# Splitting the expert gathers of a product-key layer into u rows and v rows, and taking two of nine token tiles dense

## The reference, cut to what matters

```
q = xb @ w_query                          # 8 heads x 2 halves x 128
s = q . sub_keys ; sv, si = top_k(s, 16)  # 128 keys in each half
cand = sv0 + sv1 ; fv, fi = top_k(cand, 16)
eidx = si0 * 128 + si1 at fi              # 16 experts per head
g = softmax(fv)
u = expert_u[eidx] ; a = u . xb           # (token, slot)
w = g * gelu(a)
out = sum over slots of w * expert_v[eidx]
```

## Time and profile before

| | us |
|---|---|
| median of 3 runs | 3683.47 (3682.42 to 3684.99) |
| profiled execution, its span | 3684.3 |
| before the first indirect transfer | 729.2 |
| one tile of the second part | 325.4 |

### The profile page before, as it was taken

How to read it: one execution, slowest core, us unless ns; L and a number is a source line. 1 busy time by engine, 2 the same in 40 slices (tenths; PEclk the granted TensorE clock), 3 DMA queues, 4 the chain that set the end, 5 groups by cost and what they waited for, 6 DMA issues and landing times.

```text
span 3684.3 us, 48012 instructions
## 1 busy us (share of the span) xinstructions
PE 3158.2 (86%) x17895; PEld 1389.9 (38%) x17895; DVE 2311.1 (63%) x6107; ACT 719.1 (20%) x2373; POOL 1110.6 (30%) x1177
## 2 busy tenths in 40 slices
PE   6999999889888878988887898889788888977776
PEld 3545556634334324423432343344234334422222
DVE  1333343867757866775776677677667757765444
ACT  2434434311111111111111111111111111111111
POOL 0000000033333333333333333333333333333332
PEclk8999999799999999999999999999999999999999
DMA  5000114299999999999999999999999999999997
GB/s 217 24 29 23 35 34 169 91 401 421 421 421 419 418 414 417 413 414 420 415 414 420 416 414 415 417 418 416 412 417 416 416 416 418 413 414 420 419 418 326
DMA packets 192682, 1275.60 MB, mean 346 GB/s; under 512 B 21056, under 2 KB 24768, under 8 KB 44608
## 3 DMA queue, kind: packets, MB, share of 16 engines
q0 software_dynamic: 165888, 1208.03, 79.4%
q1 hardware_dynamic: 26560, 64.49, 4.9%
HBM read 1260.12 MB, written 12.32 MB: 345 GB/s over the span
## 4 chain that ended last, share of the span: by engine, by line
DMA 46%; PE 35%; DVE 9%; issue 5%; POOL 4%; ACT 1%; SPq 0%; DVEq 0%; POOLq 0%; ACTq 0%
DMA arena<-in_experts,arena 45%; PE PS L1353 10%; PE PS L1182 8%; PE PS L1367 7%; POOL arena L651 4%; DVE arena L976 4%; PE PS L1276 3%; PE PS L1166 2%; PE PS L1399 2%; PE PS L1265 1%; PE PS L1225 1%; DVE arena L1051 1%; DVE arena L1054 1%; DVE arena L1057 1%; PE PS L1205 0%
## 5 line engine op out<-in xcount | busy, mean ns | idle before, releaser
L1353 PE MATMUL PS<-arena 128*128 128x512 bf16 x6912 | 1655.6, 382 | 453.1 <-DVE arena L976 440.6
L976 DVE CUSTOM_DVE_ANT_0 arena<-arena,PS 128x1024 f32<-128x1024 f32 x1152 | 1396.2, 1221 | 871.7 <-DMA arena<-in_experts,arena 548.4
L651 POOL DMA_INDIRECT arena<-in_experts,arena x1152 | 1089.0, 945 | 1938.0 <-PE PS L1367 1572.7
L1353 PEld LDWEIGHTS PS<-arena 128*128 128x128 bf16 x6912 | 611.5, 98 | 1480.5 <-DVE arena L976 865.1
L1367 PE MATMUL PS<-arena 128*32 128x512 f32 x4608 | 558.8, 603 | 16.8 <-ACT arena L867 16.8
L861 ACT ACTIVATE arena<-arena 128x4 f32<-128x4 f32 x288 | 59.5, 207 | 2156.2 <-DVE arena L976 2137.0
L1182 PE MATMUL PS<-arena 128*128 128x512 f32 (+1 forms) x720 | 309.8, 567 | 13.9 <-DMA arena<-in_w_in 7.9
L1399 PEld LDWEIGHTS PS<-arena 128*128 128x128 f32 x2304 | 266.6, 192 | 101.5 <-issue 101.5
L1399 PE MATMUL PS<-arena 128*128 128x128 f32 x2304 | 289.7, 280 | 0.0
L867 ACT ACTIVATE arena<-arena 128x1 f32<-128x1 f32 x1152 | 245.5, 284 | 9.4
L1367 PEld LDWEIGHTS PS<-arena 128*32 128x32 f32 x4608 | 120.8, 109 | 313.9 <-issue 175.4
(11 more groups left out here) (124 smaller groups left out, 1526.8 us busy)
## 6 DMA issues: line engine op xcount, KB each, us to landing
arena<-in_experts,arena POOLq DMA_INDIRECT x1152
arena<-in_w_in SPq DMA_DIRECT2D x8, 1024.0 KB, 11.8
arena<-in_w_query SPq DMA_DIRECT2D x4, 2048.0 KB, 16.1
arena<-in_xT SPq DMA_DIRECT2D x9, 512.0 KB, 3.9
h_scratch<-arena SPq DMA_DIRECT2D x9, 512.0 KB, 2.9
arena<-h_scratch SPq DMA_DIRECT2D x9, 512.0 KB, 8.1
out<-arena SPq DMA_DIRECT2D x9, 512.0 KB
arena<-in_x_prompt SPq DMA_DIRECT2D x8, 512.0 KB, 3.5
```

What stands on the lines that cost most here:

```text
L651: pool.indirect_dma_start(out=uv[r], out_offset=None, in_=experts, in_offset=bass.IndirectOffsetOnAxis(ap=expert_T[t % 2][:, tok:tok + 1], ...
L976: dve.tensor_tensor_reduce(uv[r][:, 0:D], uv[r][:, 0:D], xb(n), 1.0, 0.0, ALU.mult, ALU.add, a_dot[(n // 4) % 2][:, n % 4:n % 4 + 1]).then ...
L1353: mm = pe.matmul(PS[:, 2 + 2 * (n % 2) + c, :], pick[:, tok:tok + 1].broadcast_to([P, P]), parts[t % 2][k][:, 512 * c:512 * c + 512], star ...
```

## The change

It replaces the second part. Seven tiles (`D_TILES`, 0 to 6) are gathered in another way, and two (`PAIR`, 7 and 8) aren't gathered at all. The work is dealt over 256 units of four slots or four tokens, with 35 more at the end for the v side.

- **u by slot.** One indirect transfer takes, for one slot, the u rows of all 128 tokens (4 KB each, 0.5 MB). Tokens lie on the partitions, so `dot` multiplies by `xrow`, the x rows of the tile in SBUF. `spread_x` and the bf16 splits go. x rows are stored to a scratch tensor (`store_x2`) and loaded again by SP (`load_row`), h rows are loaded twice (`load_h`, `load_residual`). The routing of later tiles runs ahead of the gathers.
- **v by token.** When the 128 slots of a tile are done, gelu and gates are one operation each, PE turns the weights, and 35 units behind the u side POOL issues one indirect transfer for each token (128 v rows, 0.5 MB) into eight buffers. ACT writes the four weights of a unit in one copy (`spread_weights`). `weigh_experts` is as before.
- **Two tiles dense.** From unit 151 on, in two halves of 64 expert blocks each: 16 units in which DVE makes one-hot tiles (`spots`: four scaled comparisons of 128x128 and one of 128x256 for four tokens), PE multiplies them (`scatter`), and ACT copies the gates into the matrix `G`. Then 35 units with 64 blocks: SP streams a block of 128 experts of U (turned by the host) and of V, 0.5 MB each, into rings of three, `dense_dots` (8 matmuls of 256 columns), gelu on ACT, `gate_dense` on DVE, `dense_values` (4 matmuls of 512 columns), all float32. The u gathers end with unit 223, the v gathers with 258, the blocks with 252.

```diff
-                    for o in range(SLOTS):
-                        n = t * SLOTS + o
-                        tok = 32 * (o % 4) + o // 4
-                        r = n % RING
...
-                        if n >= RING and (n - RING) % 4 == 0:
-                            pool.wait_ge(four_used, (n - RING) // 4 + 1)
-                        pool.indirect_dma_start(
-                            out=uv[r], out_offset=None, in_=experts,
...
+                for n in range(UNITS + LAG):
+                    s, f = split(n)
+                    if s < len(D_TILES):
+                        if f == 0:
+                            pool.wait_ge(routed, s + 1)
+                        for g in range(4):
+                            m = 4 * n + g
...
+                            if m >= U_RING:
+                                pool.wait_ge(dots_ready, m - U_RING + 1)
+                            o = 4 * f + g
+                            pool.indirect_dma_start(
+                                out=u_ring[m % U_RING], out_offset=None, in_=expert_u,
...
+                    v = n - FOURS - LAG
+                    if v >= 0:
...
+                        if v >= 2:
+                            pool.wait_ge(four_used, v - 1)
+                        for g in range(4):
+                            m, tok = 4 * v + g, 32 * g + f
+                            pool.indirect_dma_start(
+                                out=e_ring[m % E_RING], out_offset=None, in_=expert_v,
...
+                def dot(s, o):
+                    n = u_slot(s, o)
+                    r = n % U_RING
+                    dve.wait_ge(u_in[r], 16 * (n // U_RING + 1))
+                    if s and o == 0:
+                        dve.wait_ge(xrow_in[s % 2], 16 * ((s + 1) // 2))
+                    dve.tensor_tensor_reduce(u_ring[r], u_ring[r], xrow[s % 2], 1.0, 0.0, ALU.mult, ALU.add,
+                                             a_dot[s % 2][:, o:o + 1]).then_inc(dots_ready, 1)
...
+                def spots(j, g):
+                    n = GROUPS * j + g
+                    if n >= 2:
+                        dve.wait_ge(scatter_psum, n - 1)
+                    t0 = P * (g // FOURS) + 4 * (g % FOURS)
+                    for k in range(4):
+                        dve.tensor_scalar(hot_j[n % 2][:, k, :], iota, j_T[:, t0 + k:t0 + k + 1], g_T[:, t0 + k:t0 + k + 1],
+                                          ALU.is_equal, ALU.mult).then_inc(hot_ready, 1)
+                    dve.tensor_tensor(hot_i[n % 2], iota[:, HALF * j:HALF * (j + 1)].unsqueeze(1).broadcast_to([P, 4, HALF]),
+                                      i_T[:, t0:t0 + 4].unsqueeze(2).broadcast_to([P, 4, HALF]), ALU.is_equal).then_inc(hot_ready, 1)
...
+                def dense_dots(b):
...
+                    if b:
+                        pe.wait_ge(act_ready, b)
+                    pe.wait_ge(uT_in[b % T_RING], 16 * (b // T_RING + 1))
+                    for k in range(KD):
+                        mm = pe.matmul(PS[:, A_BANK, 0:2 * P], uT_ring[b % T_RING][:, k, :],
+                                       x2T_pair[:, k, :], start=(k == 0), stop=(k == KD - 1))
+                    mm.then_inc(act_psum, 1)
+
+                def dense_values(b):
...
+                    pe.wait_ge(wd_ready, b + 1)
+                    pe.wait_ge(v_in[b % T_RING], 16 * (b // T_RING + 1))
+                    for q in range(2):
+                        for c in range(2):
+                            mm = pe.matmul(PS[:, ACC + 2 * q + c, :], w_ring[b % W_RING][:, P * q:P * q + P],
+                                           v_dense[b % T_RING][:, 512 * c:512 * c + 512], start=(b == 0), stop=(b == NKEYS - 1))
+                    mm.then_inc(dense_done, 1)
```

More of the change, by code:

```diff
@@ L91 @@
[L91 to L98, removed]
@@ new lines @@
+PE_AT, ACT_AT, DVE_AT = deal()
+DENSE_AT = ROUTE_AT[-1] + 25
+BURST_UNITS, BLOCK_UNITS = 16, 35
+GROUPS = 2 * P // 4
+HALF = NKEYS // 2
+DENSE = {}
+for j in range(2):
+    begin = DENSE_AT + j * (BURST_UNITS + BLOCK_UNITS)
+    for g in range(GROUPS):
+        DENSE.setdefault(begin + g * BURST_UNITS // GROUPS, []).append(("scatter", j, g))
+    for i in range(HALF):
+        DENSE.setdefault(begin + BURST_UNITS + i * BLOCK_UNITS // HALF, []).append(("block", j * HALF + i))
+DENSE_END = max(DENSE)
@@ new lines, with routes_before, weights_before, scatters_before @@
+assert DENSE_END < UNITS
+def routes_before(u):
+    return 1 + sum(ROUTE_AT[t] + 22 < u for t in range(1, NT))
+def weights_before(t):
+    return max(0, (ROUTE_AT[t] + 21) // FOURS)
+def scatters_before(u):
+    return sum(kind == "scatter" for at, events in DENSE.items() if at < u for kind, *_ in events)
+T_RING = 3
+ACT_RING, W_RING, BEHIND = 2, 4, 2
+ROUND = 12582912.0
+FINISH = D_TILES[:-1] + PAIR + D_TILES[-1:]
+COLLECT_AT = [FOURS * (s + 2) + LAG for s in range(len(D_TILES) - 1)] + [DENSE_END + 2] * 2 + [UNITS + LAG]
@@ L106 @@
+RESIDUAL_AT = [at - 8 for at in COLLECT_AT]
 FIRST_SHARE = (20, 26, 26, 10, 10, 10, 10, 48)
@@ L114 @@
     spent += STEP_LENGTH[s[0]]
-ARENA = 56000
+ARENA = 56128
 V_RING, VB_RING = 6, 3
@@ new lines, in dense_gelu, with squares @@
+                def dense_gelu(b):
+                    act.wait_ge(act_psum, b + 1)
+                    if b >= ACT_RING:
+                        act.wait_ge(wd_ready, b - ACT_RING + 1)
+                    act.activation(act_ring[b % ACT_RING], PS[:, A_BANK, 0:2 * P], ACT.Gelu)\
+                       .then_inc(act_ready, 1)
+                def squares(n):
+                    t = FINISH[n]
+                    act.wait_ge(acc_free, n + 1)
+                    tiles = sum(ROUTE_AT[r] <= COLLECT_AT[n] + 2 for r in range(1, NT))
+                    act.wait_ge(x2T_psum, tiles + 1)
+                    act.wait_ge(x2_stored, 16 * min(tiles, len(D_TILES) - 1))
+                    if n:
+                        act.wait_ge(y_ready, n)
+                    act.activation(x2_work, residual_of(t), ACT.Square, accum_out=ss2[:, 1:2]).then_inc(ssf_ready, 1)
+                    act.wait_ge(ssf_ready, n + 1)
@@ L1085, in finish @@
+                def finish(n):
+                    t = FINISH[n]
+                    dve.wait_ge(rmsf_ready, n + 1)
+                    if n == 0:
                         dve.wait_ge(gf_in, 16)
@@ new lines, in turn_weights, with scatter @@
+                def turn_weights(s):
+                    pe.wait_ge(w_ready, s + 1)
+                    pe.wait_ge(turned, routes_before(FOURS * (s + 1) + 1))
+                    if scatters_before(FOURS * (s + 1) + 1):
+                        pe.wait_ge(G_ready, scatters_before(FOURS * (s + 1) + 1))
+                    pe.transpose(PS[:, T_BANK, 2 * P:3 * P], w_sb, ident).then_inc(wT_psum, 1)
+                def scatter(u, j, g):
+                    n = GROUPS * j + g
+                    if g == 0 and j:
+                        pe.wait_ge(act_ready, HALF * j)
+                    if n >= 2:
+                        pe.wait_ge(G_ready, n - 1)
+                    if n % 2:
+                        pe.wait_ge(turned, NT)
+                        pe.wait_ge(wT_ready, (u - 1) // FOURS)
+                    pe.wait_ge(hot_ready, 5 * n + 5)
+                    for k in range(4):
+                        mm = pe.matmul(PS[:, A_BANK + n % 2, HALF * k:HALF * k + HALF], hot_j[n % 2][:, k, :], hot_i[n % 2][:, k, :],
+                                       start=True, stop=True)
+                    mm.then_inc(scatter_psum, 1)
```

664 lines of the change are left out of this document (410 added, 254 removed).

## The result

The changed kernel takes **3840.1 us** (median of 4 runs, 3828.2 to 3845.1), the kernel before 3684.2 beside it: ratio **1.0418** (95% interval 1.0401 to 1.0435). It is 4.2% slower. The forecast had 3754 us, 1.9% slower, with a range of 3590 to 3900: the sign and the range held, the size was less than half of what came.

What follows compares the result with a forecast made beforehand. POOL bound by gather waits of about 1 us a unit, PE bound at the end. Stages summed as 740 + 235 + 1288 + 394 + 627 + 429 + 28 + 13 = 3754 us, range 3590 to 3900.

Steps and rivals of the forecast that it cites:

- Bytes: Gathers and streams move 134 MB less, extra x and h traffic gives back some 13 MB; rate taken as 412 GB/s.
- Rival 4: 4 KB rows and half-size gathers are slower, 357 GB/s, 1.47 us a gather: 3910 us in all; chance 0.05.
- The lock: A POOL gather stops about 0.13 us after its start until a two-SBUF-input DVE operation ends; 0.69 and 1.05 us seen.
- Scatter units, 12.3 us: 32 units with one-hot comparisons on DVE: 9.96 us of POOL issue plus 2.3 of gather waits each, 394 us in all.
- Units 0 to 34, 235 us: Start with u gathers alone, DVE the bound: 35 x 4.7 + 65 + 5 = 235 us.
- Routing units, 11.1 us: 116 units with u, v and routing, POOL-bound with 1.1 us of waits each: 1288 us.
- Block units: Dense blocks, PE 7.0 us each: 41 units with u at 15.3 (627 us), 29 without at 14.8 (429 us).
- The signs: Gathers well over 0.95 us, POOL nearly gapless in units 35 to 166; DMA share 0.93 there, about 0.65 at the end.
- rival 1: Gathers slip into gaps between dots and POOL keeps up, 10.35 us a unit: 3604 us in all; chance 0.30.
- The second (4037, heavy waits): Random phase, or strings of dots letting no gather in: units of 12.8 and 15 us, 4037 us; chance 0.15.
- The third, the clock: Low PE clock in the block stage: over 4000 us if in a third, about 3820 in a few gaps; chance 0.05.

Runs made afterwards that it cites:

- the second experiment: Changed kernel with the second half of the columns left out of dense_values in all blocks but the first and last: 3742.5 us, ratio 1.0154.
- the first experiment: Changed kernel with its two-input dot replaced by a sum over the u row alone, one SBUF input: 3683.8 us, ratio 0.9997.

## Why the prediction was right in sign and short in size

The mechanism was right: POOL has no spare time left, and dots with two SBUF inputs hold its gathers. What failed is the size of the wait in the scatter units, and the sum for the first 35 units. Together they are 82 us, as much as the profiled execution (3836.3) lies above 3754; the other terms differ by 6 us at most and cancel.

**Bytes right, the rate a little high.** 121 MB went. Where the transfers are full, 4 KB rows in gathers of half the size ran at 404 GB/s (the first block window), 401 to 409 over all runs, where a window of the kernel before showed 416 and I took 412. Rival 4, 357 GB/s, fell, but it had the direction right, by 2 to 3%.

**The lock: right, and shown.** "A gather stops about 0.13 us after its start until such an operation has ended" came from two pairs of the earlier trace rows. Taking the second SBUF input away ended it; adding one to the kernel before brought it there. The Trainium skill ("SBUF — State Buffer", section "Who interferes with whom") has the later of the two block until the other has finished. The trace agrees for a gather that comes into a dot (345 of 351); it shows no dot that waits for a gather. The section's inference that a two-input operation doesn't hold up descriptor generation does not hold here: gathers of 0.94 us took 1.98 to 2.21 us.

**Scatter units, 12.3 us: the step that failed, 52 of the 82 us.** "Each gather waits 0.29 us in the mean (half a dot in 0.38 of cases, 0.1 otherwise)" set gathers and dots at a random phase, and averaged. The share of gathers that were held was near that, 0.39 and 0.48, but most of them waited for a whole dot and not for half of one. The time from one held gather to the next (2.50 us) is the cycle of dot and comparisons, so the phase is set, and set at its worst; 1.38 and 1.48 us are the mean gathers there, a wait of 0.44 and 0.54 us, 13.7 and 14.2 us a unit. Moving the comparisons away from between the dots, with nothing else changed, took the stage to 12.3 us, so the price that I gave to an average came out for dots that stand together (mean gathers 1.21 and 1.24 us), and not for this order. That it came out to 0.1 us is luck: there too the held gathers wait for more than half a dot.

**Units 0 to 34, 235 us: 30 short.** "DVE waiting for gathers in the middle, never in the first 35 units" was wrong. I took DVE's work as the only bound there, with u alone on POOL. In the timeline from 927 to 932 us each u gather takes 1.99 us and comes 2.29 after the one before, in step with two dots, so two gathers take as long as four dots; the gathers' mean is 1.30. Without the lock the stage takes 253.0 us, so 12 of the 30 are its work. The rest is in my other terms, by the first dots of the units: units 0 to 4 took 31.9 us where 5 x 4.7 is 23.5, units 5 to 20, in which routing is dealt, 147.8 where 16 x 8.8 is 140.8, and units 21 to 34 85.0 where 14 x 4.7 is 65.8; the 5 that I added covers a part. For the last 14 units the forecast contradicts itself: it gave 5.1 us of transfer a unit beside 4.7 of DVE, and summed 4.7. With one input they took 73.9 us, 5.3 each, so the lock's 11 us are there. What makes the first five long, no run tests.

**Routing units, 11.1 us: right, measured 11.06.** The mean gather of 1.07 us makes 8 x 0.13 = 1.0 us of waits where I had 1.1. "The three behind it fall into the gaps and wait 0.05 each" was not how: of the 20 gathers from 1500 to 1529 us four took 1.97 to 1.99 us, three 1.02 to 1.63, and thirteen 0.94 (1.20 in the mean, above the stage's 1.07). The gain from a cure was smaller than the wait, though, 0.37 us a unit, since the other limit lies at 10.69. That limit is the transfers, at more bytes and a lower rate than I had: 1240.4 us at 406 GB/s are 504 MB, 4.34 a unit where I had 10.35 us x 412 GB/s = 4.26, and the first 340 us of the stage in that run show 409 with a share of 1.03. It is read from the windows; no run changes the bytes.

```profile
1000.00:1340.00 340.00, 188.69 (x1106) 100.15 (x1106) 291.31 (x751) 25.93 (x64) 247.94 (x259) 0.72 1.03 409
```

**Block units: right.** 7.0 us a block: the rows below (start, length) begin 3.46 and 3.52 us apart. 15.2 us with u where I had 15.3, 14.9 without where I had 14.8. The time is right; with u, both resources were at the same level, and the second experiment shows that the transfers set it.

```profile
3606.96 3.62 PE L1628 MATMUL PS<-arena 128*128 128x256 f32 x16
3610.42 3.60 PE L1641 MATMUL PS<-arena 128*128 128x512 f32 x8
3613.94 1.92 PE L1593 MATMUL PS<-arena 128*32 128x512 f32 x16
```

**The signs.** POOL was busy almost without gaps, as forecast. The DMA share didn't fall as said: 1.01 for 0.93 in the routing stage, 0.80 for "about 0.65" at the end. The rates did, 391 and 274 of 412 GB/s, 0.95 and 0.67. I had taken share for rate, and the sign that was to tell this forecast from rival 1 couldn't.

**The rivals.** The first (3604, no waits) fell, and more than the waits stood against it: with them taken away 3684 was measured, not 3604, since routing units then take 10.69 us, scatter units 11.3 and the start 253 (the gathers took 959 and 950 ns, so hardly a wait is left). Even without waits the change would have gained nothing. The second (4037, heavy waits) was near on the scatter alone, 14 us for its 15, and by another way than a random phase; on routing it was wrong. The third, the clock, fell: 0.98 to 1.00 in the first and last block windows. In the windows at 0.59 to 0.71 PE is busy 19 to 69% of the time; what the low clock adds to its part of the chain there, no run tests.

**Where the gain of 294 us went.** About 156 us were lost to the lock, shown by taking it away. 98 come back when half of the float32 value matmuls is left out, 92 of them where PE runs them while the transfers idle, and the two add. Of the rest, about 200, the windows of the first experiment show the place, against 412 GB/s: 68 us in the stretch with u alone, 52 more in the last blocks, 22 in the tail, and 55 between them, where the transfers run at 382 to 406. These are the first and the last blocks:

```profile
739.60:992.60 253.00, 51.17 (x378) 48.75 (x378) 235.74 (x467) 15.27 (x25) 133.30 (x141) 0.59 0.83 302
3210.00:3641.50 431.50, 431.50 (x1757) 254.61 (x1756) 26.14 (x62) 26.72 (x87) 108.73 (x116) 1.00 0.80 274
```

## What to carry to other kernels

Before moving an operand from PSUM to SBUF, look at whether GpSimd issues indirect transfers at the same time and how much of its time is free: the same input cost nothing in a kernel with POOL half idle and 4% in one with POOL full. Where one engine holds up another, don't average over a random phase; compare the periods, for the held engine can fall into step with the one that holds it, and the order in which work is dealt decided some 60 us by itself. Read whether transfers are full from their rate and not from their share alone. When transfers are saved by computing, ask in each stage apart whether the engine that takes the work over is the bound there: half of the value matmuls was worth nothing under full transfers and 92 us behind them.

## What the runs showed of the hardware that was not expected

- An indirect gather held by a dot goes on between two dots that follow without a gap: the second dot began 0.07 us before the first ended, and the gather ended 0.81 us after the first. It is not starved in a row of dots. Behind L1185 it was: the gather at 2361.68 met L1185, which ended 0.09 us into the next dot, and it was held to the end of that dot.
- The four scaled comparisons of 128x128 float32 with operands from a column, and L1185, hold gathers little by themselves: with all of them in place and a dot of one input, the gathers of the scatter stages took 0.96 us in the mean.
- Splitting one gather of 8 KB rows into two of 4 KB rows costs POOL a whole issue more, 0.94 and 0.30 us, and the transfers 2 to 3% of their rate: 401 to 409 GB/s where rows of 8 KB had 416. An estimate from that: 4.34 MB take 10.69 us at 406 and 10.43 at 416, so some 38 us over the 148 routing and scatter units.
